# Seven transfers of zeros, issued from GpSimd's queue ahead of its wait for memory rows

## The chip, the cores and the metric

The kernel runs on one core of a Trainium2 chip. The time is that of one execution on the device, in microseconds (us), and the comparison is between the median of several executions before and after the change. The core's engines are named as in the profile: PE (TensorE, matrix multiplies, with PEld for its weight loads), DVE (VectorE), ACT (ScalarE), POOL (GpSimd) and SP (SyncE, which only issues transfers here). SP and POOL each have a DMA queue of their own; both queues are served by the same 16 DMA engines, called the ring below.

## The reference, cut to what matters

The computation is one inference step of a two-layer decoder trunk, for 512 prompt tokens and 8 sample tokens of width 1024. Layer 0 mixes with an S5 block, layer 1 with an HGRN2 block, and each layer has two SwiGLU feed-forward blocks and a cross-attention into 256 memory tokens:

```python
def swiglu(x, w_in, w_out):
    gate, up = jnp.split(x @ w_in, 2, axis=-1)
    return (jax.nn.silu(gate) * up) @ w_out

# layer i:
x = x + 0.5 * swiglu(rmsnorm(x, ffn1_norm[i]), ffn1_w_in[i], ffn1_w_out[i])
x = x + mixer(rmsnorm(x, mix_norm[i]))            # S5 in layer 0
x = x + cross_attend(rmsnorm(x, xattn_norm[i]), mem_k[i], mem_v[i], ...)
x = x + 0.5 * swiglu(rmsnorm(x, ffn2_norm[i]), ffn2_w_in[i], ffn2_w_out[i])
```

The S5 mixer is a diagonal complex recurrence over time, `h_t = lam_bar * h_(t-1) + b_bar * u_t`, `y_t = Re(c * h_t) + d * u_t`. The kernel evaluates it in chunks of `CS` = 8 steps, for which it needs tables of powers of `lam_bar` times `b_bar` and times `c`. One of them, the sequence table `s5_t`, holds for every group of 16 channels the response within a chunk. It is causal, and so a part of it is zero.

## The kernel before

The weights of every product stream from memory in tiles called `raw`, two slots (j = 0 and 1) that are refilled in turn by SP (L966). ACT copies a tile to `w_hi` (L1330), DVE computes the rest `w_lo` (L1827), and PE multiplies both with the activations (L3021 with `w_hi`, L3026 with `w_lo`). SP may refill a slot only when DVE has computed `w_lo` from it (`lo_ready`). Each engine executes its program in order, and the order of the stages is fixed: `ffn1_in0` of layer 0 (gate and up), `ffn1_out0` (the product with `ffn1_w_out`, whose tiles are 704 KB), `ffn1_in1`, `ffn1_out1`, then the S5 mixer.

Beside this stream, three things happen during the first feed-forward block of layer 0:

- **The memory rows.** ACT and DVE prepare the normed memory tokens, split in `mg_hi` and `mg_lo`, for both layers. SP writes them to the DRAM tensor `mem_split` (L929 and L931), two transfers of 1 MB for each layer; the four increments of `mem_out` tell that they have landed. The tiles of `mg_lo` lie where the tables `sFe` are put later, so POOL must not begin the tables before the rows have landed.
- **The tables.** POOL computes S5's parameters in `s5_discretize`, ending with `dD` (L1175), then waits for `mem_out` (L1178), and then makes the tables in eight rounds, a = 0 to 7. In each round, the first `table_part` writes `sFe` and the second writes `sGe` (six operations each, L736 to L738), each followed by an increment of `s5_tables`.
- **The use of the tables.** At places in PE's stream that are fixed by hand (`PREP`), `prepare` turns round a's `sFe` (L2560) and multiplies round a's `sGe` with `bZ` (L2567) and `ident` with `dD` (L2570). ACT copies the results to `sTF` and `sKst` (L1462, L1467), and SP, at places of its own (`K_OUT`), writes them to `s5_g` and `s5_t` (L936, L946). PE waits at L2567 until `s5_tables` has reached 2a + 2. The places of the rounds 0 to 3 lie in `ffn1_out0`, behind its first, second, third and fourth pair of weight tiles.

The zeros of `s5_t` come from a tile `zeros` of 128 x 128, set once at the start. Seven transfers write them, one in each of the rounds 0 to 6, issued from POOL's own queue. Transfer a reads 16 partitions and writes for each of them 64 runs of 16(7 - a) floats, so 448 bytes for a = 0, 384 for a = 1, down to 64 for a = 6; the runs lie 1 KB apart in DRAM. The semaphore `s5_zeros_out` is waited on much later, by SP in `s5_loads`, ahead of the S5 mixer.

Of the kernel before, what the change touches and what calls it, by code (L numbers as in the profile page):

```python
# [28 lines left out]
SG, SC, SP_, CS = 64, 16, 64, 8  # L29
# [105 lines left out]
def trunk_kernel(nc, i_, o_):  # L135
# [16 lines left out]
    def at(name, shape, dtype, offset):  # L152
        return nc.alloc_sbuf_tensor_at(name, shape, dtype, offset=offset)
# [56 lines left out]
    zeros = at("zeros", [P, P], F32, o_zeros)  # L210
# [166 lines left out]
    s5_t = nc.dram_tensor("s5_t", (P, SG, 256), F32, kind="Internal").ap()  # L377
# [27 lines left out]
    def sem(name):  # L405
        return nc.alloc_semaphore(name)
# [30 lines left out]
    s5_k_out, s5_zeros_out = sem("s5_k_out"), sem("s5_zeros_out")  # L437
# [291 lines left out]
    def table_part(eng, link, out, n, m, signs, j0, j1, tmp):  # L729

        shape = [P, j1 - j0, n, SC]
        pv = [pw[:, e, 0:n, j0:j1].rearrange("p d j -> p j d").unsqueeze(3).to_broadcast(shape) for e in range(2)]
        mv = [m[:, e, j0:j1].unsqueeze(2).to_broadcast(shape) for e in range(2)]
        tmp = tmp[:, 0:(j1 - j0) * n * SC].rearrange("p (j d c) -> p j d c", j=j1 - j0, d=n)
        for e, sign in enumerate(signs):
            link(eng.tensor_tensor(out[:, e], pv[0], mv[e], ALU.mult))  # L736
            link(eng.tensor_tensor(tmp, pv[1], mv[1 - e], ALU.mult))  # L737
            link(eng.tensor_tensor(out[:, e], out[:, e], tmp, sign))  # L738

    block = nc.Block()  # L740
    with block:
# [275 lines left out]
        def _(pool):  # L1017
# [88 lines left out]
            def s5_discretize():  # L1106
# [56 lines left out]
                for g in range(2):  # L1163
                    rows = slice(64 * g, 64 * g + 64)
                    for e in range(2):
# [9 lines left out]
                link(pool.tensor_tensor(dD[:], fold[:, 96:112].unsqueeze(1).to_broadcast([P, KD, SC]),  # L1175
                                        vec[:, V_D:V_D + KD].unsqueeze(2).to_broadcast([P, KD, SC]), ALU.mult))
                pool.wait_ge(consts_done, 4)
                pool.wait_ge(mem_out, 16 * 2 * DEPTH)  # L1178
                for a in range(8):
                    if a < CS - 1:  # L1180
                        n = SC * (CS - 1 - a)
                        pool.dma_start(s5_t[SC * a:SC * (a + 1), :, 0:n],
                                       zeros[0:SC, 0:n].unsqueeze(1).to_broadcast([SC, SG, n]))\
                            .then_inc(s5_zeros_out, 16)
                    table_part(pool, link, sFe[a], CS, bBar, (ALU.subtract, ALU.add), 4 * a, 4 * a + 4, sTmp)
                    pool.nop().then_inc(s5_tables, 1)
                    if a >= 2:
                        pool.wait_ge(s5p_fill, S5P.at("K", a - 2) + 1)
                        pool.wait_ge(s5_g_out[a % 2], 16 * 2 * (a // 2))
                    table_part(pool, link, sGe[a % 2], CS + 1, cT, (ALU.add, ALU.subtract), 4 * a, 4 * a + 4, sTmp)  # L1190
                    pool.nop().then_inc(s5_tables, 1)
# [108 lines left out]
            for n in range(len(ST)):  # L1300
                if ST[n][:2] == ("ffn1_in0", 0) and s5_norm is not None:
                    s5_discretize()
                if ST[n][:2] == ("ffn1_out1", 0):
                    rotations()
                    squares(n, norm_after[ST[n][:2]])
                    s5()
                    continue
                if ST[n][:2] == ("ffn1_out1", 1):
                    hgrn_constants()
                if ST[n][0] == "hg_in":  # L1310
                    hg_in()
                if ST[n][0] == "xo":
                    attend(ST[n][1])
                if ST[n][:2] in norm_after:
                    squares(n, norm_after[ST[n][:2]])
                if ST[n][:2] == ("ffn1_in0", 1):
                    kv_low(1)
# [1869 lines left out]
```

## Time before and how to read the profile

| what | value |
| --- | --- |
| median of 3 runs | 2360.91 us (2357.8 to 2361.16) |
| span of the profiled execution, first to last instruction | 2357.9 us |
| PE busy | 2332.7 us (99%) |
| DVE, ACT, POOL busy | 1295.9, 869.0, 609.4 us |
| POOL queue's transfers | 560 packets, 1.84 MB |
| SP queue's transfers | 477856 packets, 280.66 MB |

The profile is that of one execution. Its rows give the start of a piece of work in us from the start of the span, its duration, the engine, the line of the kernel, and the operation as output <- inputs. What stands in brackets at the end of a row is how long the engine had been idle and what ended the idle time. "PEclk" is the granted TensorE clock as a share of 2.4 GHz. "DMA share" is the mean busy share of the 16 DMA engines; it can pass 1.00 since the packets of one engine overlap a little.

### The profile page before, as it was taken

What the parts mean: (1) busy time and instruction counts of PE and PEld (TensorE: products, weight loads), DVE (VectorE), ACT (ScalarE), POOL (GpSimd) and SP (SyncE); (2) the same over time, 40 slices, a digit from 0 to 9 for tenths busy, and PEclk for the clock granted to TensorE, in tenths of its full rate; (3) what the DMA queues carried; (4) which work ended last, traced back from release to release, by engine and by line L of the source; (5) the groups of instructions that cost most, each with busy time, mean ns of one, the idle gap of its engine ahead of it and who ended that gap; (6) DMA issues with size and microseconds to landing.
All of it is one profiled execution on the core that took longest, in us unless ns stands there. A gap on an engine that the chain in (4) does not pass through costs nothing.

```text
span 2357.9 us, 50146 instructions
## 1 busy us (share of the span) xinstructions
PE 2332.7 (99%) x21043; PEld 2270.3 (96%) x21043; DVE 1295.9 (55%) x1906; ACT 869.0 (37%) x1399; POOL 609.4 (26%) x591
## 2 busy tenths in 40 slices
PE   8999999999999999999999999999999999999999
PEld 8999999889979999999999999999999979999999
DVE  6653643964576443445543344577777666443443
ACT  4422333453233321322433233267775233321323
POOL 4779967331103000004111010432122102000003
PEclk9999999999999999999999999999999999999999
DMA  6455445553562333333543333233332653333332
GB/s 167 128 161 149 123 134 169 171 170 107 166 242 84 98 99 91 96 96 99 158 117 111 100 108 115 83 100 108 104 111 77 213 188 91 97 94 94 98 94 94
DMA packets 483707, 289.19 MB, mean 123 GB/s; under 512 B 22289, under 2 KB 466962, under 8 KB 482514
## 3 DMA queue, kind: packets, MB, share of 16 engines
q1 hardware_dynamic: 477856, 280.66, 40.4%
q0 software_dynamic: 560, 1.84, 0.6%
q10 hardware_dynamic: 5122, 4.25, 0.5%
q8 instruction: 129, 2.11, 0.4%
q14 instruction: 40, 0.33, 0.0%
HBM read 258.86 MB, written 27.85 MB: 122 GB/s over the span
## 4 chain that ended last, share of the span: by engine, by line
PE 90%; DVE 4%; POOL 2%; ACT 1%; issue 1%; DMA 1%; SPq 0%; DVEq 0%; POOLq 0%; ACTq 0%
PE lin L3021 51%; PE lin L3026 25%; PE mis L2512 4%; POOL sTmp L737 1%; PE mis L2650 1%; PE lin L2600 1%; PE lin L2762 1%; PE mis L2633 1%; PE lin L2757 1%; PE lin L2983 1%; POOL sGe L738 0%; DVE w_lo L1827 0%; POOL sFe L738 0%; PE lin L2650 0%; PE mis L2626 0%
## 5 line engine op out<-in xcount | busy, mean ns | idle before, releaser
L1827 DVE TENSOR_TENSOR w_lo<-raw,w_hi 128x1024 fp32r<-128x1024 f32 (+1 forms) x322 | 464.0, 1441 | 294.4 <-ACT w_hi L1330 293.7
L1330 ACT ACTIVATE w_hi<-raw 128x1024 fp32r<-128x1024 f32 (+1 forms) x328 | 365.1, 1113 | 314.2 <-PE lin L3026 244.4
L3021 PE MATMUL lin<-a_rear,w_hi 128*128 128x264 f32 x3552 | 455.6, 279 | 0.0
L3021 PE MATMUL lin<-a_front,w_hi 128*128 128x256 f32 x3552 | 451.5, 279 | 1.1 <-DVE a_rear L1840 0.7
L3021 PEld LDWEIGHTS lin<-a_rear,w_hi 128*128 128x128 f32 x3552 | 432.6, 188 | 0.0
L3021 PEld LDWEIGHTS lin<-a_front,w_hi 128*128 128x128 f32 x3552 | 424.4, 188 | 4.5 <-issue 1.8
L3026 PE MATMUL lin<-a_rear,w_lo 128*128 128x264 f32 x1776 | 245.1, 278 | 0.0
L3026 PE MATMUL lin<-a_front,w_lo 128*128 128x256 f32 x1776 | 240.5, 277 | 1.0 <-DVE w_lo L1827 1.0
L2391 DVE SCALAR_TENSOR_TENSOR xT<-lin,xT 128x520 f32<-128x520 f32 (+1 forms) x87 | 60.9, 700 | 322.8 <-PE lin L3026 322.1
L1063 POOL TENSOR_TENSOR acc<-xT 128x520 f32<-128x520 f32 x8 | 12.2, 1521 | 864.6 <-DVE xT L2391 836.6
L3026 PEld LDWEIGHTS lin<-a_rear,w_lo 128*128 128x128 f32 x1776 | 223.8, 188 | 0.0
L3026 PEld LDWEIGHTS lin<-a_front,w_lo 128*128 128x128 f32 x1776 | 219.5, 188 | 1.6 <-DVE w_lo L1827 1.6
L1741 ACT ACTIVATE f_front<-t 128x256 fp32r<-128x256 f32 (+1 forms) x88 | 36.9, 419 | 398.1 <-DVE t L2372 398.1
L3021 PE MATMUL lin<-f_rear,w_hi 128*128 128x264 f32 x1386 | 179.8, 283 | 0.0
L3021 PEld LDWEIGHTS lin<-f_rear,w_hi 128*128 128x128 f32 x1386 | 172.1, 189 | 0.1
L3021 PE MATMUL lin<-f_front,w_hi 128*128 128x256 f32 x1386 | 170.3, 276 | 0.0
L3021 PEld LDWEIGHTS lin<-f_front,w_hi 128*128 128x128 f32 x1386 | 163.3, 188 | 0.1
L1737 ACT ACTIVATE t<-t 128x520 f32<-128x520 f32 x88 | 56.5, 642 | 270.7 <-DVE t L2366 270.7
L2370 DVE TENSOR_TENSOR t<-lin,rstd 128x520 f32<-128x520 f32 x88 | 61.6, 700 | 161.3 <-PE lin L3026 161.3
L1067 POOL TENSOR_TENSOR sqt<-xT 128x520 f32 (+1 forms) x54 | 82.0, 1518 | 210.9 <-DVE xT L2391 148.8
L3021 PE MATMUL lin<-g_all,w_hi 128*128 128x264 f32 (+1 forms) x1024 | 128.8, 278 | 0.0
L3021 PEld LDWEIGHTS lin<-g_all,w_hi 128*128 128x128 f32 x1024 | 122.8, 188 | 1.1 <-DVE g_all L1967 1.1
(512 smaller groups left out, 3181.5 us busy)
## 6 DMA issues: line engine op xcount, KB each, us to landing
raw<-in_ffn_w_in_dram SPq DMA_DIRECT2D x176, 512.0 KB, 3.9
raw<-in_ffn_w_out_dram SPq DMA_DIRECT2D x64, 704.0 KB, 4.6
kc<-in_cache_mem_k_dram SPq DMA_DIRECT2D x32, 512.0 KB, 7.1
vc<-in_cache_mem_v_dram SPq DMA_DIRECT2D x16, 1024.0 KB, 9.1
raw<-in_hg_w_in_dram SPq DMA_DIRECT2D x32, 512.0 KB, 4.3
raw<-in_xattn_w_kv_dram SPq DMA_DIRECT2D x16, 512.0 KB, 4.4
raw<-in_s_w_glu_dram SPq DMA_DIRECT2D x16, 512.0 KB, 4.0
raw<-in_xattn_w_q_dram SPq DMA_DIRECT2D x16, 512.0 KB, 3.9
```

What stands on the lines that cost most here:

```text
L737: link(eng.tensor_tensor(tmp, pv[1], mv[1 - e], ALU.mult))
L1067: step.link(pool.tensor_tensor(sqt[:], tile(xT, m), tile(xT, m), ALU.mult))
L1330: act.activation(w_hi[:, j, 0:kt, :], raw[:, j, 0:kt, :], ACT.Copy).then_inc(hi_ready, 1)
L1737: act.activation(t2[:], t1[:], ACT.Silu).then_inc(gate_out, 1)
L1741: ins = act.activation(tile(out, i), t3[:, cols], ACT.Copy)
L1827: dve.tensor_tensor(low_weights(n, j), raw[:, j, 0:kt, :], w_hi[:, j, 0:kt, :].bitcast(F32), ALU.subtract).then_inc(lo_ready, 1)
L2370: step.link(dve.tensor_tensor(t4[:], lflat(1), rstd[:], ALU.mult))
L2391: dve.scalar_tensor_tensor(out=tile(xT, m), in0=lflat(j), scalar=scale, in1=tile(xT, m), op0=ALU.mult, op1=ALU.add)\
L2512: ins = pe.matmul(kv_bank(c)[:, 0:NM], w[:, e, k, :], x[:, k, :], start=k == 0 and u == 0, stop=k == KD - 1 and u == 2)
L2600: ins = pe.matmul(lin[32 * h:32 * h + NS, 1, 0, 0:NM], pZ[:, t, h, b, :], vc[layer][V_SLOT[b]][:, t, h * NM:(h + 1) * NM], start=False, st ...
L3021: pe.matmul(lpart(j, half), high[:, k, :], (x_lo if u else x_hi)[half][:, k, :], start=start and u == 0 and k == 0, stop=False)
L3026: ins = pe.matmul(lpart(j, half), low[:, k, :], x_hi[half][:, k, :], start=False, stop=k == kt - 1)
```

## The change

The loop that issues the zeros is taken out of the table rounds and put in front of the wait for the memory rows. The transfers themselves, the tables and every wait stay as they are.

```diff
                 pool.wait_ge(consts_done, 4)
+                for a in range(CS - 1):
+                    n = SC * (CS - 1 - a)
+                    pool.dma_start(s5_t[SC * a:SC * (a + 1), :, 0:n],
+                                   zeros[0:SC, 0:n].unsqueeze(1).to_broadcast([SC, SG, n]))\
+                        .then_inc(s5_zeros_out, 16)
                 pool.wait_ge(mem_out, 16 * 2 * DEPTH)
                 for a in range(8):
-                    if a < CS - 1:
-                        n = SC * (CS - 1 - a)
-                        pool.dma_start(s5_t[SC * a:SC * (a + 1), :, 0:n],
-                                       zeros[0:SC, 0:n].unsqueeze(1).to_broadcast([SC, SG, n]))\
-                            .then_inc(s5_zeros_out, 16)
                     table_part(pool, link, sFe[a], CS, bBar, (ALU.subtract, ALU.add), 4 * a, 4 * a + 4, sTmp)
                     pool.nop().then_inc(s5_tables, 1)
```

## Rows read from the trace of the kernel before

**Rows 1.** The page: the span, and the queue of POOL's transfers.

```profile
span 2357.9 us, 50146 instructions
...
q0 software_dynamic: 560, 1.84, 0.6%
```

**Rows 2.** Timeline of PE, 141 to 206 us: start, duration, work, idle before.

```profile
141.34 2.20 PE L3021 MATMUL lin<-f_front,w_hi 128*128 128x256 f32 x18
...
146.17 1.31 PE L3026 MATMUL lin<-f_front,w_lo 128*128 128x256 f32 x9 [0.46 <-DVE w_lo L1827]
...
191.57 1.03 PE L2560 MATMUL mis<-ident,sTF 128*128 128x128 f32 x8
195.46 0.64 PE L2567 MATMUL mis<-sGe,bZ 128*32 128x128 f32 x16 [2.85 <-POOLq L1191]
...
196.08 4.48 PE L3021 MATMUL lin<-f_rear,w_hi 128*128 128x264 f32 x22
...
205.44 2.78 PE L3021 MATMUL lin<-f_rear,w_hi 128*128 128x264 f32 x22
```

**Rows 3.** Windows: one microsecond behind PE's wait; PEclk stands third from the end.

```profile
197.00:198.00 1.00, 1.00 (x7) 1.00 (x6) 0.00 (x0) 0.76 (x1) 0.92 (x2) 0.50 1.19 205
```

**Rows 4.** Timeline of POOL, 123 to 275 us.

```profile
123.69 0.40 POOL L1175 TENSOR_TENSOR dD<-sTmp,vec 128x128 f32<-128x128 f32 x1
135.65 1.01 POOL L1182 DMA_DIRECT2D s_t<-zeros  x1 [11.56 <-DMA mem_split<-mg_lo]
...
156.20 0.79 POOL L1182 DMA_DIRECT2D s_t<-zeros  x1 [0.66 <-POOL sGe L738]
...
192.54 2.71 POOL L738 TENSOR_TENSOR sGe<-sGe,sTmp 128x576 f32<-128x576 f32 x1
...
274.92 1.11 POOL L736 TENSOR_TENSOR sFe<-pw,bBar 128x512 f32<-128x512 f32 x1 [0.18 <-POOL sGe L738]
```

**Rows 5.** The chain that ended last: the piece ahead of POOL's first transfer.

```profile
127.86 7.08 DMA mem_split<-mg_lo
```

**Rows 6.** Timeline of SP's queue, 124 to 136 us: transfers as they are issued.

```profile
125.20 0.37 SPq L966 DMA_DIRECT2D raw<-in_ffn_w_in_dram  x1
...
127.86 0.34 SPq L931 DMA_DIRECT2D mem_split<-mg_lo  x1
...
129.49 5.84 SPq L966 DMA_DIRECT2D raw<-in_ffn_w_out_dram  x2
```

**Rows 7.** Transfer issued at 129.49: KB and us from issue to landing.

```profile
raw<-in_ffn_w_out_dram SPq DMA_DIRECT2D x1, 704.0 KB, 8.0
```

**Rows 8.** Timeline of ACT: its copy of that tile.

```profile
137.49 1.39 ACT L1330 ACTIVATE w_hi<-raw 128x1408 fp32r<-128x1408 f32 x1
```

**Rows 9.** Windows: the last two numbers are DMA share and GB/s.

```profile
125.00:126.00 1.00, 1.00 (x11) 1.00 (x10) 1.00 (x3) 0.19 (x1) 0.00 (x0) 1.00 0.00 0
...
128.00:130.00 2.00, 2.00 (x20) 2.00 (x19) 1.23 (x1) 0.20 (x1) 0.00 (x0) 1.00 1.06 426
```

**Rows 10.** POOL's queue in 138:142.2, 157:162, 177:181 and 197:201 us: packets, MB, share.

```profile
q0 software_dynamic: 125, 0.46, 64.6%
...
q0 software_dynamic: 112, 0.39, 68.8%
...
q0 software_dynamic: 88, 0.32, 72.6%
...
q0 software_dynamic: 80, 0.26, 67.8%
```

**Rows 11.** Both queues in 178:180.4 us; then loads issued at 177.04 and 146.1 us.

```profile
q0 software_dynamic: 59, 0.24, 100.9%
q1 hardware_dynamic: 30, 0.01, 3.0%
...
raw<-in_ffn_w_out_dram SPq DMA_DIRECT2D x1, 704.0 KB, 8.3
...
raw<-in_ffn_w_out_dram SPq DMA_DIRECT2D x1, 704.0 KB, 4.8
```

## The prediction, made before the changed kernel ran

> **What bounds the kernel now.** I read the page first. PE is busy for nearly the whole span, so a change on POOL can only pay where PE waits. The timeline of PE shows one wait for POOL. At 191.57 us PE turns round 2's table; it is done at 192.60 and starts the product with `sGe` only at 195.46, after 2.85 us of idleness [rows 2]. Its releaser is the increment behind the last operation of round 2's `sGe`, which ran from 192.54 to 195.25 [rows 4].
>
> The wait costs more than its length. The next 22 products took 4.48 us, where the same form took 2.78 us at 205.44 [rows 2], and the granted clock was 0.50 of full speed there (1.2 GHz instead of 2.4) [rows 3]. PE had idled before it fell. So the wait is worth 2.85 + 1.70 = 4.55 us.
>
> POOL is late because it started late. It was through with `dD` at 124.09 and sat idle for 11.56 us, until `mg_lo` had landed [rows 4]; that piece of the chain ends at 127.86 + 7.08 = 134.94 [rows 5]. The second question is what the ring does meanwhile. It is idle from 125 to 126 us and full from 128 to 130 [rows 9]. SP issues four things in that stretch: a tile at 125.20, the two halves of the memory rows, the second at 127.86, and the first 704 KB tile of `ffn1_out0` at 129.49 [rows 6].
>
> **What leaves POOL's rounds.** Up to the end of round 2, three transfers go. The first took POOL from 134.94 to 136.66; without it the table can start some 0.1 us after the landing, so 1.6 us are gained. For the second, POOL idled 0.66 us and issued for 0.79, which makes 1.45; round 7, which has no transfer, has a gap of 0.18 there [rows 4]. The gain is 1.27, and I take the same for the third. The sum is 1.6 + 2 x 1.27 = 4.1 us. If the memory rows landed when they do now, round 2's `sGe` would end at 191.1, PE would see it at 191.3 and not wait at all: it arrives at 192.60. The whole 4.55 us would be gained. The other four transfers are worth 5 us of POOL's time, at nothing: the view of PE's waits puts no other wait down to POOL up to the S5 mixer.
>
> **What the issues cost where they stand now.** Seven times 1.45 us from 124.09 end at 134.2, inside the idle time. The bounds are 7 x 0.79, ending at 129.6, and 7 x 1.72, ending at 136.1, which is 1.2 us too late. Since PE would have 1.3 us to spare, the issues themselves cost nothing.
>
> **What the transfers cost where they run now.** This is the term that decides. Over the whole execution, POOL's queue kept the ring busy for 0.6% of 2357.9 us, which is 14.1 us [rows 1], for only 1.84 MB. For the first four transfers the windows give 64.6% of 4.2 us = 2.7, 68.8% of 5 us = 3.4, 72.6% of 4 us = 2.9 and 67.8% of 4 us = 2.7, together 11.8 us [rows 10]; 2.4 us are left for the last three. Today they are spread over 120 us. After the change they are all issued between 124.7 and about 134 us, on a ring that has one idle microsecond there.
>
> How do the two queues share the ring? At 177.04 SP issued a tile load while transfer 2 was running. In 178:180.4 POOL's queue had 100.9% of the ring and SP's 3.0%, and the load took 8.3 us to land, where one of the same size, issued at 146.1, took 4.8 [rows 11]. The 3.5 us of delay are about the 2.9 us of that transfer. So a zero transfer that is ahead holds back a load for all of its own time. I take it that the ring serves the queues about in the order of issue.
>
> POOL's issues would start at 124.75, 126.2, 127.65 and 129.1. Three of them (9.0 us of ring) are ahead of `mg_lo` at 127.86, and four (11.8 us) are ahead of the tile at 129.49 [rows 4, 6].
>
> - **The tile.** It landed at 129.49 + 8.0 = 137.49 [rows 7], ACT copied it until 138.88 [rows 8], and PE used the copy at 141.34 [rows 2], so the slack is 2.46 us. With 11.8 us more, PE starts 9.3 us late. DVE's half of the tile, for which PE waits 0.46 us today at 146.17 [rows 2], is then ready in time: 8.9 us. PE stands idle for some 9 us, so the clock falls again, and I add 1.7 us. The tile issued at 125.20 is behind transfer 0 alone; what PE loses for it is inside the same 9 us and not added.
> - **The memory rows.** POOL's round 2 is ready for PE at 191.3 + 9.0 = 200.3.
> - **The meeting.** PE arrives at its old waiting place at 192.60 + 8.9 + 1.7 = 203.2, so POOL is no longer late. Before, PE was there at 195.46 and lost 1.70 behind it, which makes 197.16.
>
> The sum is 203.2 - 197.16 = +6.0 us. On the profiled execution's span of 2357.9 [rows 1] this is 2363.9. Its own whole time isn't shown; the median of the runs stands 3.0 us above the span, and I take the difference from there: 2360.9 + 6.0 = 2366.9 us. In short, the change is +D - 5.8 for a tile that lands D late, once D is above 2.5; for POOL's side to decide instead, the memory rows would have to be later than by D.
>
> What is behind the tile: the next tile of the pair has at least 6 us more of slack, since PE uses it only after its products with the first, which last from 141.34 to 147.48 at least [rows 2], and SP issues it when DVE is through with its slot. Everything behind PE then moves together.
>
> **A rule of the skill that differs.** The Trainium skill, page "DMA: Bandwidth & Descriptors", section "Queues, rings and completion order", says that each DMA engine takes turns between its queues, a packet at a time. Rows 11 agree only in part: 59 packets of one queue went beside 30 of the other. By that rule the result is the second rival below.
>
> **The rivals.**
>
> 1. *Nothing is held back that matters (ends on the other side).* SP's queue is served first once it has work, and the zeros fill what is left. At most transfer 0, which finds the ring idle, is ahead: 2.7 us. The tile's slack of 2.46 covers it, and POOL is ready at 191.3 + 2.7 = 194.0, so PE waits 1.4 us, perhaps without a fall of the clock. The gain is 4.55 - 1.4 = 3.2 us; with the rows on time it is 4.55. That gives 2356.4 to 2357.7 us. For it speaks the volume: the zeros are 1.84 MB in small pieces. Against it speak rows 11, where a load did not get past a zero transfer. It decides below D = 5.8.
> 2. *Turns by packet.* With equal turns, the small packets of the loads wait for a large one of zeros each time. The 14.1 us of zeros are then all out before the memory rows and the tile: D = 14.1 for both. PE's side gives 14.1 - 5.8 = +8.3; POOL's side gives 191.3 + 14.1 = 205.4 against PE's arrival at 205.5, so no more. 2369.2 us.
> 3. *Larger turns.* Each queue gets about one transfer of zeros against a longer run of the other. Two or three transfers (6.1 to 9.0 us) are ahead of the tile: +0.3 to +3.2, or 2361.2 to 2364.1 us.
> 4. *The slowest engine decides.* The shares are means over 16 engines, and a load has landed when its last engine is through. The four windows in which the transfers ran are 17.2 us long together instead of 11.8. D = 17.2 gives +11.4, 2372.3 us.
>
> **How the numbers follow.** A change of 0.2% is 4.7 us, about what a measurement of this kernel can tell from none. The forecast (in the order of issue, D of 10.5 to 13.5, +4.7 to +7.7) has 0.32. Rival 2 has 0.15, rival 4 has 0.10, rival 3 has 0.18, rival 1 has 0.25. Slower by over 0.2%: 0.32 + 0.15 + 0.10 = 0.57, less 0.03 for runs that fall short: 0.54. Faster by over 0.2% is barely within reach, since the whole wait is worth 4.55 us; a quarter to a third of rival 1, for small gains elsewhere, gives 0.07. The same: 0.39. The range takes rival 1's lower end and stops short of rival 4: 2356.4 to 2371.5. The likeliest case alone is 2365.6 to 2368.6.
>
> **What would show each step.** In the new profile, seven issues of POOL stand between 124.7 and 134 us without a table operation between them, and the rounds have gaps of 0.2 us. The piece of the chain for `mg_lo`, 7.08 us today, is 16 us long; the tile issued at 129.49 takes near 20 us to land instead of 8.0; PE has a new idle time of about 9 us near 141 us, waiting for ACT's copy, with a clock of 0.50 behind it; and the wait of 2.85 us at L2567 is gone. The prediction is wrong if the tile lands within 2.5 us of its old time, or if `mg_lo` does and the tile does not. It is also wrong in size if the zeros take much less of the ring in a batch than they did one by one.

## The result, and the profile after

The change made the kernel slower. The median of five executions went from 2360.23 us (2357.80 to 2361.16) to 2374.68 us (2373.55 to 2379.32); the ratio is 1.0069, with a 95% interval of 1.0058 to 1.0079. The direction and the place are those of the prediction (2366.9 us), the size is not: about +14 us instead of +6, above the range. The profiled execution took 2378.16 us, of which the span is 2376.4 us. That is 18.5 us more than the span of [rows 1]. In this execution all work is 1.24 us later from the start (`dD` at 124.93 instead of 123.69), which has to be taken off each comparison of starts. It arose in the first 13 us, ahead of all that was changed: eight products with `xin` took 1.97 us there instead of 1.09.

POOL's timeline after, to be set beside [rows 4]. The seven issues are in the idle time, as meant:

```profile
124.93 0.40 POOL L1175 TENSOR_TENSOR dD<-sTmp,vec 128x128 f32<-128x128 f32 x1
125.65 5.57 POOL L1180 DMA_DIRECT2D s_t<-zeros  x7 [0.32 <-POOL dD L1175]
156.06 1.09 POOL L736 TENSOR_TENSOR sFe<-pw,bBar 128x512 f32<-128x512 f32 x1 [24.84 <-DMA mem_split<-mg_lo]
...
174.53 1.11 POOL L736 TENSOR_TENSOR sFe<-pw,bBar 128x512 f32<-128x512 f32 x1 [0.18 <-POOL sGe L738]
```

They take 0.80 us each, and POOL then waits 24.84 us for `mg_lo` instead of 11.56. The gaps between rounds are 0.18 us. SP's queue after, to be set beside [rows 6]:

```profile
128.53 0.34 SPq L929 DMA_DIRECT2D mem_split<-mg_hi  x1
129.11 3.19 SPq L931 DMA_DIRECT2D mem_split<-mg_lo  x1
132.35 3.73 SPq L966 DMA_DIRECT2D raw<-in_ffn_w_out_dram  x1
```

The second row is new: the issue of `mg_lo` held SP up for 3.19 us, where it took 0.34. So the tile behind it is issued 1.6 us later than before, too. The view of DMA issues in 122:134 gives sizes and us from issue to landing ([rows 7] has the tile's 8.0, [rows 5] the 7.08 of `mg_lo`):

```profile
mem_split<-mg_hi SPq DMA_DIRECT2D x1, 1024.0 KB, 21.3
mem_split<-mg_lo SPq DMA_DIRECT2D x1, 1024.0 KB, 26.9
raw<-in_ffn_w_out_dram SPq DMA_DIRECT2D x1, 704.0 KB, 26.4
...
s_t<-zeros POOLq DMA_DIRECT2D x1, 448.0 KB, 7.5
s_t<-zeros POOLq DMA_DIRECT2D x1, 384.0 KB, 11.1
...
s_t<-zeros POOLq DMA_DIRECT2D x1, 64.0 KB, 26.6
```

Everything is in flight together and lands together: the last zeros at about 157, `mg_lo` at 156.0, the tile at 158.8. The windows show the ring full, and slow. Where it moved 426 GB/s before [rows 9], it now moves (last two numbers: DMA share, GB/s; PEclk ahead of them):

```profile
128.00:130.00 2.00, 2.00 (x20) 2.00 (x19) 1.40 (x3) 1.45 (x3) 2.00 (x4) 1.00 0.95 97
130.00:132.00 2.00, 2.00 (x19) 2.00 (x19) 1.05 (x2) 0.00 (x0) 1.22 (x2) 1.00 0.94 124
...
148.00:150.00 2.00, 0.00 (x0) 0.00 (x0) 0.00 (x0) 0.00 (x0) 0.00 (x0) 0.50 0.88 146
```

By queue (packets, MB, share of the ring), first over the whole execution from the page, beside [rows 1], then in 136:146, when only the zeros and the memory rows are under way:

```profile
q0 software_dynamic: 560, 1.84, 0.8%
```

```profile
q0 software_dynamic: 181, 0.60, 75.6%
q1 hardware_dynamic: 131, 1.03, 27.6%
```

The same 560 packets keep the ring busy for 0.8% of the span, about 19 us, instead of 14.1. (The page rounds to 0.1%, which is 2.4 us; the share in 122:170 gives 19.2 us, and the one in 130:270 of the kernel before 14.1.) At last PE, to be set beside [rows 2]; ACT's copy of the tile, first, answers to [rows 8]:

```profile
158.82 1.38 ACT L1330 ACTIVATE w_hi<-raw 128x1408 fp32r<-128x1408 f32 x1 [20.27 <-DMA raw<-in_ffn_w_out_dram]
```

```profile
141.57 1.09 PE L3026 MATMUL lin<-a_rear,w_lo 128*128 128x264 f32 x8
160.25 3.96 PE L3021 MATMUL lin<-f_front,w_hi 128*128 128x256 f32 x18 [17.59 <-ACT w_hi L1330]
...
211.40 1.03 PE L2560 MATMUL mis<-ident,sTF 128*128 128x128 f32 x8
212.36 0.64 PE L2567 MATMUL mis<-sGe,bZ 128*32 128x128 f32 x16
...
228.38 1.03 PE L2560 MATMUL mis<-ident,sTF 128*128 128x128 f32 x8
231.20 0.64 PE L2567 MATMUL mis<-sGe,bZ 128*32 128x128 f32 x16 [1.78 <-POOLq L1191]
231.63 0.26 PE L2570 MATMUL mis<-dD,ident 128*32 128x16 f32 x8
231.82 2.76 PE L3021 MATMUL lin<-a_front,w_hi 128*128 128x256 f32 x12
```

The account of the 18.5 us has these terms:

- 1.24 for the start, and 17.59 for the wait for the tile, less 0.46 for DVE's half, now ready;
- 1.76 for the clock of 0.50 behind the wait (3.96 instead of 2.20 us for the first 18 products);
- less 4.55 for round 2's wait and the fall of the clock behind it, both gone;
- 1.78 for a new wait, for round 3, less the 0.33 us for which PE waited there before (for ACT's copy of `sTF`);
- 1.57 for the clock, which falls behind that wait too: the first 24 products take 4.51 us (231.82 to 236.33), where they took 2.94 before.

The sum is 18.6.

### The profile page after: what moved, and what is told of

The parts are those of the page before. It is cut to its first block, busy times and chain, and to the rows that moved or that the text cites. A ratio compares the mean times of both kernels' runs of the same rounds, so it can differ in the third digit from the quotient of the medians.

```text
span 2376.4 us, 50146 instructions
## 1 busy us (share of the span) xinstructions
PE 2335.8 (98%) x21043; PEld 2273.6 (96%) x21043; DVE 1289.5 (54%) x1906; ACT 869.2 (37%) x1399; POOL 607.9 (26%) x591
## 3 DMA queue, kind: packets, MB, share of 16 engines
q0 software_dynamic: 560, 1.84, 0.8%
## 4 chain that ended last, share of the span: by engine, by line
PE 88%; DVE 4%; POOL 3%; DMA 2%; ACT 2%; issue 1%; SPq 0%; DVEq 0%; POOLq 0%; ACTq 0%
PE lin L3021 50%; PE lin L3026 25%; PE mis L2512 3%; DMA mem_split<-mg_lo 1%; POOL sTmp L737 1%; PE mis L2650 1%; PE mis L2633 1%; POOL sGe L738 1%; PE lin L2600 1%; PE lin L2983 1%; POOL sFe L738 0%; POOL sGe L736 0%; PE lin L2650 0%; DMA raw<-in_xattn_w_kv_dram 0%; PE lin L2762 0%
## 5 line engine op out<-in xcount | busy, mean ns | idle before, releaser
L3021 PE MATMUL lin<-f_front,w_hi 128*128 128x256 f32 x1386 | 171.9, 278 | 17.6 <-ACT w_hi L1330 17.6
```

Source lines behind the costliest of these rows:

```text
L3021: pe.matmul(lpart(j, half), high[:, k, :], (x_lo if u else x_hi)[half][:, k, :], start=start and u == 0 and k == 0, stop=False)
```

## The experiments

Two things were to be settled: which part of the change costs what, and why the zeros hold the ring so much longer. The theories for the second: their destination (small runs, 1 KB apart), POOL's queue and the turns of the queues, or the source and its sheer bytes. The letters in the quoted expectations stand for theories that each expectation names or takes over from one before it. In the diffs below, `zeros_out(b)` stands for the transfer of zeros number b, exactly as before. Left out are the lines that only define it, and those that declare the scratch tensor `s5_junk` and make `s5_loads` wait for fourteen transfers where there are fourteen. The diffs are against the kernel after, k_split's against the kernel before. "Front" is the place ahead of the wait for the rows. All kernels are compared with the kernel before in the same series. The table has the median, the ratio with its interval, PE's wait for ACT's copy of the first 704 KB tile, and the landing time of `mg_lo`.

| kernel | zeros in front | us | ratio | tile wait | `mg_lo` |
| --- | --- | --- | --- | --- | --- |
| before | none | 2359.3 to 2360.2 | 1 | none | 7.1 |
| after | seven | 2374.68 | 1.0069 (1.0058 to 1.0079) | 17.6 | 26.9 |
| b_late | none | 2356.60 | 0.9989 (0.9980 to 0.9998) | none | 7.1 |
| j_late4 | none | 2356.35 | 0.9984 (0.9975 to 0.9993) | none | 7.0 |
| n_tiny | seven issues of 16 KB | 2356.44 | 0.9988 (0.9979 to 0.9997) | none | 7.5 |
| d_first | one | 2360.50 | 1.0006 (0.9997 to 1.0015) | 1.5 | 11.2 |
| e_three | three | 2369.62 | 1.0042 (1.0029 to 1.0056) | 10.0 | 18.9 |
| g_tail | none, seven at the end | 2372.61 | 1.0052 (1.0038 to 1.0066) | none | 7.2 |
| c_contig | seven, adjoining destination | 2373.19 | 1.0059 (1.0045 to 1.0072) | 16.3 | 25.7 |
| o_spq | seven, from SP's queue | 2376.00 | 1.0069 (1.0055 to 1.0082) | 18.9 | 8.9 |
| h_spread | seven, source 0, 8, ..., 120 | 2368.57 | 1.0038 (1.0025 to 1.0052) | 11.9 | 21.6 |
| hc_spread | c_contig with that source | 2368.21 | 1.0036 (1.0022 to 1.0049) | 10.9 | 20.4 |
| p_spq_spread | o_spq with that source | 2368.03 | 1.0037 (1.0023 to 1.0051) | 7.8 | 7.3 |
| q_step2 | seven, source 0, 2, ..., 30 | 2367.78 | 1.0028 (1.0017 to 1.0040) | 9.1 | 18.7 |
| r_step7 | seven, source 0, 7, ..., 105 | 2368.44 | 1.0037 (1.0023 to 1.0052) | 10.9 | 20.4 |
| s_halves | fourteen halves | 2362.86 | 1.0017 (1.0007 to 1.0026) | 7.0 | 12.0 |
| i_spread | none, source 0, 8, ..., 120 | 2355.78 | 0.9981 (0.9972 to 0.9990) | none | 7.0 |
| k_split | one, rounds start earlier | 2354.33 | 0.9976 (0.9967 to 0.9985) | none | 7.5 |
| ks_late4 | none, rounds start earlier | 2356.36 | 0.9988 (0.9979 to 0.9997) | none | 4.3 |

**The gain alone: b_late and j_late4.** The zeros leave the rounds 0 to 2 (b_late) or 0 to 3 (j_late4), but go nowhere near the memory rows.

```diff
                 for a in range(8):
-                    if a < CS - 1: ...
+                    if 3 <= a:          # j_late4: 4 <= a, zeros_out(a - 4)
+                        zeros_out(a - 3)
...
+                for b in (5, 6):        # j_late4: (4, 5, 6)
+                    zeros_out(b)
```

> The transfers of zeros 0 to 4 are issued in the table rounds 3 to 7, one in each, and 5 and 6 behind round 7; none is in front of the wait for the memory rows. Theory 1 (in front, the zeros fill the ring of DMA engines and hold back SP's transfers; one at a time behind round 2 they meet only tiles with slack): PE's wait of 2.85 us and the 1.70 us of slow clock behind it go, 4.5 us faster than before, near 2355.7 us. Theory 2 (the zeros cost wherever they are not in the first three rounds, since they then meet tighter tiles): no gain, within 2 us of before or slower.

> The same places as the run with the spread source (0 to 3 in the rounds 4 to 7, 4 to 6 behind round 7), but with the narrow source, partitions 0 to 15. If one transfer at a time meets tiles with slack, equal to the spread source: 4 to 5 us faster than before. If three in a row behind round 7 hold back a tile (0.39 MB at 97 GB/s, 4 us of ring): 1 to 3 us of that is lost again.

Round 2's wait is gone in both. They gain 3.2 and 3.4 us, less than the 4.5 that was expected of b_late and the 4 to 5 of j_late4. b_late shows what the prediction did not see, a wait at round 3's place:

```profile
211.10 0.64 PE L2573 MATMUL mis<-sGe,bZ 128*32 128x128 f32 x16 [1.83 <-POOLq L1195]
```

PE's places for the rounds 2 and 3 lie 17.0 us apart (211.40 and 228.38 in the kernel after), POOL's rounds 19.4 (their `sGe` end at 211.64 and 231.00). Without the wait for round 2, PE comes to round 3 earlier, and POOL is behind there. In j_late4 round 3 has no transfer either, and PE waits 0.80 us for ACT's copy of `sTF` there, not for POOL. The clock stays at 1.00 in both, so a wait of 1.83 us does not always bring it down, and b_late pays only the wait.

**The issues alone: n_tiny.** Seven issues of 16 KB each stand in front and write to a scratch tensor; the real zeros go as in j_late4.

```diff
+                for b in range(CS - 1):
+                    pool.dma_start(s5_junk[SC * b:SC * (b + 1), 0:2 * P].rearrange("p (r c) -> p r c", r=2),
+                                   zeros[0:SC, :].unsqueeze(1).to_broadcast([SC, 2, P]))...
                 pool.wait_ge(mem_out, 16 * 2 * DEPTH)
```

> In front of the wait stand seven issues with almost no volume (16 KB each, two runs of 512 bytes from each of 16 partitions, to a scratch tensor); the real zeros are issued in the rounds 4 to 7 and behind round 7. Theory 1 (the ring's time costs, not the issues): equal to the run with the same late places and nothing in front, about 3.5 us faster than before, memory rows landed within 1 us of their old 7.1 us. If seven issues of POOL's queue as such hold back SP's, slower than before by 3 us or more.

The gain, 2.9 us, is j_late4's 3.4 within the noise, and `mg_lo` lands 0.4 us later than before. The issues cost nothing; it is the bytes behind them.

**One and three in front: d_first and e_three.**

```diff
+                for b in range(3):      # d_first: zeros_out(0) alone
+                    zeros_out(b)
                 pool.wait_ge(mem_out, 16 * 2 * DEPTH)
                 for a in range(8):
-                    if a < CS - 1: ...
+                    if 3 <= a < CS - 1: # d_first: 1 <= a
+                        zeros_out(a)
```

> Only transfer 0 stands in front of the wait; 1 to 6 stay in their rounds. Theory 1, with the rate that the changed kernel shows (448 KB at 97 GB/s, 4.6 us of ring): memory rows 4.6 us late, POOL 3.0 us late on net at round 2, PE waits 3 us more than before: about 3 us slower. With the time that the transfer took in its round (2.7 us): about 1 us slower. If zeros in front hold nothing back: 1.6 us faster.

> Transfers 0 to 2 in front of the wait, 3 to 6 in their rounds. They hold 1.15 MB of the 1.84 MB; at the 97 GB/s of the changed kernel that is 12 us of ring. Theory 1: the tile lands 12 us late, PE waits 9 us for it with 1.7 us of slow clock behind, round 2 is not waited for: 12 - 5.8 = about 6 us slower than before. If only what is behind the third transfer costs, no slower than with one in front (0 to 1 us).

One transfer of 448 KB in front delays `mg_lo` by 4.1 us. PE waits 1.47 us for the tile, and POOL's late start costs it three waits, 1.31, 2.85 and 2.14 us in the rounds 1, 2 and 3. So nothing of the gain is left; the span of the profiled execution is 2.9 us longer than before, as the first theory has it, though the medians show no difference (+0.7 us). Round 2's wait is as long as in the kernel before:

```profile
198.49 0.65 PE L2572 MATMUL mis<-sGe,bZ 128*32 128x128 f32 x16 [2.85 <-POOLq L1196]
```

But the clock doesn't fall behind it: it stays at 1.00, and the next 22 products take 2.88 us instead of the 4.48 of [rows 2]. The 1.70 us for the clock are therefore not paid in every execution, which would fit the gains of 3.2 and 3.4 us instead of 4.55; how often they are paid was not measured.

Three transfers, 1.18 MB or 64% of the bytes, delay `mg_lo` by 11.8 us, as expected. The kernel is 10.3 us slower, not the 6 expected:

```profile
152.45 4.14 PE L3027 MATMUL lin<-f_front,w_hi 128*128 128x256 f32 x18 [10.04 <-ACT w_hi L1336]
```

With the slack of 2.46 this wait means a tile that is 12.5 us late, and 12.5 - 5.8 = 6.7. The rest is round 3: PE waits 1.99 us for POOL there, the clock falls to 0.50, and this takes about 3 us more. The delay goes with the bytes: 4.1/0.46 and 11.8/1.18 give 8.9 and 10.0 us for a megabyte, and 19.8/1.84 for all seven gives 10.8.

**All seven where no rows are: g_tail.**

```diff
                 for a in range(8):
-                    if a < CS - 1: ...
...
                     pool.nop().then_inc(s5_tables, 1)
+                for b in range(CS - 1):
+                    zeros_out(b)
```

> All seven stand behind round 7, where POOL is about to idle for 13 us. Theory 1 (any seven in a row fill the ring for 14 to 19 us and hold back the tiles of the stage that runs then): PE has a new wait of 5 to 12 us near 290 to 310 us, and the kernel is 0 to 8 us slower than before. Theory 2 (the cost in front comes from the memory rows and the tile behind them in one queue, not from the seven in a row): no new wait, 4.5 us faster. It also shows what the seven take of the ring without writes of memory rows beside them.

It loses nearly as much as the change itself, 12.8 us where at most 8 were expected, some 165 us later, with no memory rows and no wait for POOL. The timeline of SP's queue says how. Kernel before, then g_tail, the writes of round 6's table and the load behind them; then PE's wait in g_tail:

```profile
294.31 4.58 SPq L946 DMA_DIRECT2D s_t<-sKst  x8
298.93 16.39 SPq L966 DMA_DIRECT2D raw<-in_ffn_w_in_dram  x4
```

```profile
294.04 24.33 SPq L946 DMA_DIRECT2D s_t<-sKst  x8
318.41 13.89 SPq L966 DMA_DIRECT2D raw<-in_ffn_w_in_dram  x4
```

```profile
325.24 3.78 PE L3025 MATMUL lin<-a_front,w_hi 128*128 128x256 f32 x16 [15.45 <-ACT w_hi L1334]
```

Eight issues that took 4.58 us take 24.33 while the zeros are on the ring (its share is 1.00 in 300:304, for 93 GB/s), and the next load starts 19.5 us late; PE idles 15.5 us. So the batch is costly at both places where it was tried, and the memory rows are not needed for it.

**The destination: c_contig.** The seven in front write the same bytes to adjoining places of a scratch tensor, in runs of 512 bytes, instead of runs of 64 to 448 bytes that lie 1 KB apart; the real zeros go as in b_late.

```diff
+                    pool.dma_start(s5_junk[SC * b:SC * (b + 1), 0:64 * n].rearrange("p (r c) -> p r c", r=64 * n // P),
+                                   zeros[0:SC, :].unsqueeze(1).to_broadcast([SC, 64 * n // P, P]))...
```

> In front of the wait stand seven transfers of the same bytes to a scratch tensor, in runs of 512 bytes that lie next to each other, instead of runs of 448 to 64 bytes that lie 1 KB apart; the real zeros are issued as in the run before (one in each of the rounds 3 to 7, two behind). If the small scattered runs are what makes the zeros slow on the ring (97 GB/s in the changed kernel), 1.84 MB take about 6 us at the 300 GB/s of other transfers, the tile lands about 6 us late, and the kernel is within 2 us of before. If the volume alone costs, or the mere fact that seven issues stand in front, it is as slow as the changed kernel, 12 to 16 us over before.

I had taken the scattered runs to be the cause. They aren't: it is 13.4 us slower than before, the changed kernel 14.5. Queues in 128:130:

```profile
q0 software_dynamic: 39, 0.16, 97.2%
q1 hardware_dynamic: 42, 0.02, 3.6%
```

0.16 MB in 2 us at 97.2% of the ring, so 80 GB/s, where loads reach 426 [rows 9].

**The queue: o_spq and p_spq_spread.** SP issues the seven transfers itself, ahead of the second pair of row writes; the second kernel also has the spread source of h_spread below.

```diff
                     l = MEM_PARK[at_]
+                    if l:
+                        sp.wait_ge(consts_done, 4)
+                        for b in range(CS - 1): ...   # sp.dma_start, the same seven transfers
                     sp.wait_ge(mem_hi, KD * (l + 1))
```

> The seven transfers are issued by SP, in its own queue, directly ahead of the second pair of memory rows; none from POOL. Theory A (narrow source and volume: the zeros take 17 to 19 us of ring from any queue): rows and tile land 17 us late or more, 12 to 16 us slower than before, like the changed kernel. Theory B (a good part of the delay comes from POOL's queue beside SP's, from packets by turns and engines that finish apart): clearly less, 2 to 8 us slower than before.

> The seven transfers from SP's own queue ahead of the second pair of memory rows, with the spread source (partitions 0, 8, ..., 120). From POOL's queue, the spread source still left the tile 13 us late. Theory C (the rest is two queues beside each other: the packets of the rows grow from 315 to 450 to 550 ns, and engines finish at different times): in one queue the zeros take 6 to 8 us alone, rows and tile land 6 to 8 us late, the kernel is 0 to 3 us slower than before. Theory D (the rest is the volume written to memory): rows and tile land 13 us late here too, 8 to 9 us slower than before.

SP's queue in o_spq, then in p_spq_spread:

```profile
129.28 20.49 SPq L932 DMA_DIRECT2D s_t<-zeros  x7
149.82 0.75 SPq L936 DMA_DIRECT2D mem_split<-mg_hi  x1
150.61 0.73 SPq L938 DMA_DIRECT2D mem_split<-mg_lo  x1
```

```profile
124.89 10.37 SPq L932 DMA_DIRECT2D s_t<-zeros  x7
135.31 1.85 SPq L936 DMA_DIRECT2D mem_split<-mg_hi  x1
```

Almost alone on the ring and on the other queue, the zeros need the same 20 us, 90 GB/s. The rows behind them then land in 8.9 us. With the spread source it is 10 us, 177 GB/s. So neither POOL's queue nor the sharing makes the zeros slow; their source does. The view of windows in o_spq shows in 131:151 that the share of the ring (second to last) says little of this rate (last):

```profile
131.00:151.00 20.00, 14.10 (x123) 13.89 (x121) 7.14 (x11) 3.21 (x5) 0.00 (x0) 0.95 0.61 107
```

From SP's queue the same bytes keep the ring busy for 0.61 of the time only, from POOL's (the kernel after, 128:132) for 0.94 to 0.95, at about the same rate. The median of p_spq_spread, 2368.03, is h_spread's, though its profiled execution (2361.91) is the fastest of its five, and the others reach 2370.11: what the choice of queue is worth with a spread source stays open.

**The source: h_spread, hc_spread, q_step2, r_step7, s_halves.** All in front, from POOL's queue. A partition is one of the 128 rows of the on-chip memory. Which 16 partitions of `zeros` are read makes no difference to what is written. The groups of the expectations are four neighbouring partitions each; they are counted by the map that the expectation of q_step2 names, where 32 to 63 count with 0 to 31, and 96 to 127 with 64 to 95, so there are 16.

```diff
-                                   zeros[0:SC, 0:n]...
+                                   zeros[0:P:P // SC, 0:n]...      # h_spread, hc_spread (on c_contig)
+                                   zeros[0:2 * SC:2, 0:n]...       # q_step2
+                                   zeros[0:7 * SC - 6:7, 0:n]...   # r_step7
+                                   # s_halves: two transfers of 8 partitions each,
+                                   # zeros[0:32:4, 0:n] and zeros[64:96:4, 0:n]
```

> The changed kernel with one edit: each transfer of zeros reads the partitions 0, 8, 16, ..., 120 of the zeros tile instead of the partitions 0 to 15. Theory 3 (all sixteen DMA engines read from neighbouring partitions of the on-chip memory, and this side is the limit of 97 GB/s, since runs next to each other at the destination did not help): the packets of zeros take near 300 ns instead of 720, the seven take 6 to 8 us of ring, the tile lands 6 to 8 us late instead of 21, and the kernel is 0 to 3 us slower than before or a little faster. Theory 4 (POOL's queue itself, with its software-made descriptors, is slow): packets stay at 700 ns and the kernel is 13 to 16 us slower than before.

> The run with seven transfers to a scratch tensor in adjoining runs of 512 bytes in front (and the real zeros, from partitions 0 to 15, in the rounds 3 to 7 and behind), with the sources of the seven in front spread over partitions 0, 8, ..., 120. Theory 3: packets of 4096 bytes at or below 250 ns, 5 us of ring, the tile 3 to 5 us late, within 2 us of before, 11 us or more faster than the same with the narrow source. Theory 4: no difference from the narrow source, 13 us slower than before. If the scattered runs cost something of their own, this run's packets are faster than those of the spread source with scattered runs.

> All seven transfers of zeros in front of the wait, as in the changed kernel, but read from every second of 32 neighbouring partitions (0, 2, ..., 30) instead of 16 neighbouring ones. With partitions 0, 8, ..., 120 the zeros took 9.5 us of the ring (0.4%) instead of 19 (0.8%), and the kernel 2368.6 us instead of 2374.7. Theory 'groups': partitions are served in groups of four, so 16 neighbours are 4 groups, while 0, 2, ..., 30 are 8 groups, as many as 0, 8, ..., 120 reach; then this run is as that one: 2367 to 2370 us, PE's wait 11 to 13 us, POOL's queue 0.4%. Theory 'distance': only sources far apart are quick, and 32 neighbours are nearly as slow as 16; then 2372 to 2375 us, a wait of 15 to 18 us, 0.7 to 0.8%. The Trainium skill, page 'SBUF — State Buffer', section on the DMA port swizzle, has a map of 16 ports by which the 16 neighbours reach 4 ports and both spread sources 8; by it the first theory holds.

> The same, read from partitions 0, 7, 14, ..., 105. If groups of four are served side by side, but partitions 32 to 63 share with 0 to 31, and 96 to 127 with 64 to 95, this source reaches 14 of 16 groups, two of them twice, where 0, 8, ..., 120 reaches 8, all twice. Theory 'sum': what counts is the number of groups reached; the zeros take 19 x 4/14 = 5.4 us of the ring, PE waits 5 to 8 us, 2361 to 2365 us. Theory 'busiest': the group that is read twice sets the time: as with 0, 8, ..., 120, so 2367 to 2370 us. Theory 'pieces': with a spread source the number of small runs is the limit, not the source: also 2367 to 2370 us, and the next run tells these two apart.

> Each transfer of zeros is cut in two with 8 partitions each, 0, 4, ..., 28 and 64, 68, ..., 92, so that each of the 16 groups is read once by each pair; 14 issues of some 0.8 us end near 136 us, when the memory rows have just landed. Theory 'sum' and theory 'busiest' both: the zeros take about 19/4 = 4.8 us of the ring or, each half being alone on it for its time, 9.5 in all but in smaller portions; the issues, 0.8 us each for 64 to 224 KB, then leave gaps that the rows use: PE waits 2 to 6 us for the tile, 2357 to 2364 us. Theory 'pieces': the 7168 small runs need the same ring time as with any spread source, 9.5 us or more, all ahead of the tile: 2366 to 2370 us.

The page's row of POOL's queue for h_spread and q_step2, which is the same, and for r_step7:

```profile
q0 software_dynamic: 560, 1.84, 0.4%
```

```profile
q0 software_dynamic: 560, 1.84, 0.3%
```

The time of the ring is halved by any of them. In 122:170 it is 9.0, 10.0 and 7.5 us, against 19.2 in the kernel after. Set against the kernel before in their own series, the kernels are 7.6 to 8.8 us slower, where the changed one is 14.5 slower. That is in between what the two theories of h_spread named (0 to 3, or 13 to 16), and hc_spread was expected within 2 us of before and is at 8.4: with the quicker packets PE still waits 9 to 12 us for the tile, and why so much is left is not shown.

q_step2 rules out distance: every second of 32 neighbours does as well as 0, 8, ..., 120. The 4 groups of 0 to 15 against the 8 of both spread sources fit this. So would a rule by which neighbouring partitions hinder each other, since no spread source has two neighbours; no run tells the two apart. r_step7, which reaches 14 groups instead of 8, lowers the queue's share once more but not the time. Windows of r_step7 show why the share no longer tells:

```profile
132.00:134.00 2.00, 2.00 (x20) 2.00 (x19) 1.10 (x1) 0.87 (x1) 0.00 (x0) 1.00 0.99 337
...
142.00:144.00 2.00, 0.00 (x0) 0.00 (x0) 0.19 (x1) 0.00 (x0) 0.00 (x0) 1.00 0.44 130
```

The ring is quick at first, and then half idle, while the tile (landed at 150.2) is still under way. It may be that some of the 16 engines are through and others aren't; no view here shows them one by one. s_halves, which reads each group once and hands its bytes over in fourteen portions over 11.30 us, is the best of those with everything in front. It still loses 0.17% (the medians differ by 2.7 us), with a wait of 7.0 us for the tile. The time is the one expected by groups (2357 to 2364 us), not the one expected by small pieces (2366 to 2370), though the wait is above the 2 to 6 us named with it; but it changes the number of issues and their spacing as well, so the busiest group is not shown to be the cause in r_step7.

**Spread source, late: i_spread.** j_late4 with the source of h_spread.

> Transfers 0 to 3 in the rounds 4 to 7, 4 to 6 behind round 7, with the spread source. No transfer is left in the rounds for which PE waits (2 and 3): both waits gone, 4 to 5 us faster than before.

2355.78 against 2356.35, with intervals that overlap: where the zeros collide with nothing that is due, the source is not to be seen in the time.

**The idle time used otherwise: k_split and ks_late4.** `sFe` of the rounds 0 and 1 lies where `mg_lo` of the first pair was, and only from round 2 on where the second pair of row tiles is still being read. So the rounds 0 and 1 can start once the first pair has landed. k_split leaves the zeros where they were; ks_late4 combines this with j_late4.

```diff
-                pool.wait_ge(mem_out, 16 * 2 * DEPTH)
+                pool.wait_ge(mem_out, 16 * 2)
                 for a in range(8):
+                    if a == 2:
+                        pool.wait_ge(mem_out, 16 * 2 * DEPTH)
```

> The zeros stay in their rounds as before; POOL waits in front of round 0 only for the first pair of memory rows (long landed) and for the second pair in front of round 2. POOL's rounds begin 11 us earlier, so PE's wait for round 2 and its slow clock go (4.5 us), but transfer 0 is now issued where the changed kernel issues it, ahead of rows and tile. By the run with transfer 0 alone in front, the tile costs PE 1.5 us: 3 us faster than before. If only the wait for POOL counts: 4.5 us faster. If the start of the rounds does not matter: no change.

> The split wait (rounds 0 and 1 wait for the first pair of rows alone) and the zeros in the rounds 4 to 7 and behind (narrow source). The split wait alone was 5 us faster than before and late zeros alone 3.4 us. Both take the same wait from PE, so no sum is expected: 5 to 6 us faster than before, equal to the split wait within 1 us.

POOL's timeline in k_split, and PE at round 2's place:

```profile
125.06 1.01 POOL L1184 DMA_DIRECT2D s_t<-zeros  x1 [0.32 <-POOL dD L1175]
126.10 1.13 POOL L736 TENSOR_TENSOR sFe<-pw,bBar 128x512 f32<-128x512 f32 x1
```

```profile
192.34 1.03 PE L2562 MATMUL mis<-ident,sTF 128*128 128x128 f32 x8
193.30 0.64 PE L2569 MATMUL mis<-sGe,bZ 128*32 128x128 f32 x16
```

The tables start 10.6 us earlier (126.10; before, one us behind the transfer at 135.65 [rows 4]), PE waits for POOL nowhere, and the clock does not fall there. The gain is 5.0 us, 0.24% (interval 0.15 to 0.33%): the whole of the 4.55 us, and the lowest median of all, though the interval overlaps those of i_spread and j_late4. It has a cost of its own: with POOL at work, DVE's two operations that make the last of `mg_lo` take 2.77 us together instead of 0.88, and the rows go out later (SP issues `mg_lo` at 131.51; the slack holds it). Taking the zeros out of the rounds as well, ks_late4, adds nothing; it gains 3.7 us, where 5 to 6 were expected. No wait for POOL was left to remove, and there is a wait of 2.0 us for ACT's copy of a tile at 217.12 that the others don't have, whose cause was not followed up.

## Why the prediction was right in direction and wrong in size

**Right.** The wait and its price, 2.85 + 1.70 us: k_split and j_late4 take it away and gain 5.0 and 3.4, so the size holds roughly; the 1.70 for the clock isn't paid each time (d_first). The issues cost nothing (n_tiny). The mechanism holds: the batch in front of the rows delays the tile and, through it, PE; the slack of 2.46 us, the 0.46 us of DVE's half and the 1.7 us of clock came out as written: D is 158.82 - 137.49 - 1.24 = 20.1 us, PE waited 17.59 = 20.1 - 2.5, and the first products lost 1.76. With this D the prediction's own formula, +D - 5.8, gives +14.3 us, and the medians differ by 14.45. That the two meet is in part luck. The profiled execution lost 18.5 - 1.24 = 17.3 us, which is 14.3 and the 3.0 of round 3, a term that the formula hasn't got; D in the other executions is not known.

**The step that failed is the size of D, 11.8 us, in "What the transfers cost where they run now".** It has two parts.

- *Four transfers ahead of the tile, in order of issue.* The issues were put at 1.45 us each, a gap that also held other things; they took 0.80, the lower bound of [rows 4]. Five had started at 129.11, when `mg_lo` was issued, and all seven before the tile at 132.35, which SP's blocked issue had delayed further. And the ring does not go by order of issue: in 136:146 it took 181 packets of one queue and 131 of the other. That is rival 2's mechanism. By the Trainium skill, page "DMA: Bandwidth & Descriptors", section "Queues, rings and completion order", each DMA engine takes turns between its queues by the packet; the trace after agrees as far as both queues moved side by side. For the tile both orders come to the same, since all seven were ahead of it: D = 14.1, so +8.3.
- *The ring time of a transfer, as busy share times length.* This is the rest, 14.1 against 20.1. In the batch the same packets kept the ring busy for 19.2 us. The four windows of [rows 10] are 17.2 us long for 1.44 MB, so 84 GB/s; at this rate 1.84 MB take 21.9 us. The share was no measure of what a transfer costs, because the transfers were bound by their source: one by one from POOL's queue they showed 14.1 us, in a batch 19.2, from SP's queue a ring at 0.61 of its time, and each time the bytes moved at 80 to 97 GB/s. Rival 4 had the right reading (length, not share), for only four transfers; its 2372.3 us is the nearest to the measured 2374.68.

**Also missed.** The prediction let POOL's side decide only if the rows were later than by D. But POOL's rounds are 2.4 us longer than the distance of PE's places, so with round 2's wait gone, round 3 is the tight one, even with the rows on time (b_late: 1.83 us). In the profiled execution it cost 1.78 + 1.57, less the 0.33 of before; e_three paid about as much, and its 10.3 us are the formula's 6.7 with it. Executions in which it does not bring the clock down could explain the lower ones of the five (2373.6 to 2374.7 against 2378 and 2379), but only one was profiled. The prediction's 3.0 us between the span and the whole time is off as well: in the runs after it is 1.7 to 1.8.

**The signs it named.** The seven issues (125.65 to 131.22 us) and the gaps of 0.2 us: right. `mg_lo` 16 us long: 26.9. The tile near 20 us: 26.4. An idle time near 9 us: 17.6, with the clock at 0.50 behind it as said. Round 2's wait: gone.

## What to carry to other kernels

Price a transfer that is to be moved by its bytes over the rate it reached when it ran alone, not by its busy share, and sum over all that will be in flight together; then look at what is due on every queue meanwhile, also at how long the issuing instruction itself will block. A narrow source (here 16 neighbouring partitions) can fill the ring at a quarter of the rate of a load (97 against 426 GB/s); if the data is constant, read it from partitions that are spread (8 groups instead of 4 halved the time here, 14 gained no more), and issue it where nothing is due. An engine's idle time is better filled with work that doesn't need what the others are waiting for: splitting the wait (k_split) gained 5 us where filling it with transfers lost 14. When one wait is removed, look at the next place too: here round 3 was tighter than round 2.

## What the runs showed of the hardware that was not expected

- **A source of 16 neighbouring partitions is slow on the whole ring.** 80 to 97 GB/s from POOL's queue for scattered and adjoining destinations (the kernel after, c_contig), 20 us for 1.84 MB from SP's (o_spq, 90 GB/s); about half the time from partitions 0, 8, ..., 120 (p_spq_spread, 177 GB/s) or 0, 2, ..., 30. The Trainium skill, page "SBUF — State Buffer", section "Door 1: The DMA port swizzle (why `[64,N]` ≈ `[32,N]`)", maps partitions to 16 ports by groups of four: 0 to 15 reach 4 ports, each of the two spread sources 8. At the page's 435 GB/s for all 16 that would be an estimated 109 and 218 GB/s. The runs agree in the ratio of two and stay below both (90 and 177 GB/s). That r_step7, with 14 ports by the map, took no less time than 8 is not explained.
- **An issue can block.** SP's issue of `mg_lo` took 3.19 us instead of 0.34 with the zeros in front, and eight small writes 24.33 us instead of 4.58 (g_tail). POOL's own issues stayed at 0.80 us each.
- **The clock falls after a short wait in some places and not in others.** Behind 1.78 us of idleness at round 3 in the kernel after and 1.99 us in e_three it went from 1.00 to 0.50; behind 1.83 us in b_late and 1.78 us in r_step7, at the same place, it stayed at 1.00. At round 2 it fell behind 2.85 us in the kernel before and stayed behind 2.85 us in d_first. No run tells what differs.
